# Streaming the tokens of three feed-forward products in blocks of 16, 128 and 4 from both halves in turn

## Chip, cores and metric

The kernel runs on one core of one Trainium2 chip. The metric is the device time in microseconds (us) of one execution. The kernel before takes 1833.14 us, the median of two runs (1832.73 and 1833.56 us).

## What is computed

A two-layer diffusion trunk over 256 latent tokens and 256 context tokens, width 1024. Each layer has a feed-forward half step, a pair of parallel mixers (attention and a short convolution) and a second feed-forward half step. The change touches only the first product of the feed-forward steps:

```python
def swiglu(h, wi, wo):
    a, g = jnp.split(h @ wi, 2, axis=-1)
    return (jax.nn.silu(g) * a) @ wo
...
    x = x + 0.5 * mod[:, 2] * swiglu(modulate(rmsnorm(x, norm_w[0]), mod[:, 0], mod[:, 1]), ffn1_wi, ffn1_wo)
    xc = xc + 0.5 * modc[2] * swiglu(modulate(rmsnorm(xc, norm_w[0]), modc[0], modc[1]), ffn1_wi, ffn1_wo)
```

`wi` is 1024 x 5632 (2816 value columns `a`, 2816 gate columns `g`), `wo` is 2816 x 1024, all float32. There are four such steps. In the first three both streams go through (512 tokens), in the fourth only the 256 latent tokens.

## The kernel before

The program is written engine by engine, each engine's order by hand, with semaphores between them; no scheduler or planner moves anything.

**Data.** The activations lie transposed: `hH` and `hL` are [128, 8, 512], channel in the partition, eight chunks of channels, 512 tokens along the row: tokens 0 to 255 are the latent half, 256 to 511 the context half. A float32 value is kept as a high part (`hH`, type float32r) and a low part (`hL`), and so are the weights (`wH`, `wL`). A product is three matmuls, high by high, low by high and high by low: the helper `triple`, lines 585 to 587. In a matmul here the weights are the stationary operand (a weight load of 128x128, the engine PEld of the profile) and the tokens are the moving operand, up to 512 columns. The result goes to a PSUM bank, which holds exactly 512 float32 columns per partition, token by token.

**Weights.** SP loads pieces of 512 KB into a ring of four slots, `raw`. ScalarE rounds a piece to `wH` (line 1071), VectorE subtracts to get `wL` (line 1355), TensorE uses it; `w_used` frees the slot.

**The stage of the change.** For feed-forward step `f` (0 to 3), `ffn` runs eleven groups of 256 value and 256 gate columns. The first group is `opening` (lines 642, 644, 654), which works with the norm before it and is not touched. Groups 1 to 10 are `group(i)`: four calls of `columns_piece`, one for each piece of weights. Each call goes over four channel chunks `kk` and two output banks and makes one `triple` for each, so 24 matmuls. The value product goes to banks 0 and 1, the gate product to banks 2 and 3. Their readers, on ScalarE and VectorE, take the banks after the last matmul, in token order. The steps 0, 1 and 2 of this count lie at 55.4 to 278.34, 743.54 to 966.47 and 1114.73 to 1337.66 us, with 960 matmuls of 512 columns each; step 3 (256 columns a matmul, tokens kept at 112 to 367 of the row) is at 1654.65 to 1764.34 us. Between every second group of steps 0 to 2 stand eight short records of `ada_reduce` (line 616), part of the modulation vectors.

**Other lines named below.** Line 956 weighs the values of the attention: its moving operand is `PT[:, 2 * r:2 * r + 2, kb * P:(kb + 1) * P]`, two runs of 128 columns out of two rows of `PT`; it gives 64 output columns for each `r`, and the two `r` run side by side. Line 598 is a small product at the start whose moving operand is one run of 256 columns and which runs four side by side. Both are float32, and a float32 matmul leaves two records in the trace. `last_rows` is the end of the feed-forward's second product, done by halves of 256 tokens.

Of the kernel before, what the change touches and what calls it, by code (L numbers as in the profile page):

```python
# [83 lines left out]
def span(t):  # L84

    at = SHORT_AT if t == SEQ else 0
    return slice(at, at + t)
# [32 lines left out]
def ada_batch(f, which):  # L120

    return next((b for b, (g, w, _, _) in enumerate(ADA_BATCHES) if (g, w) == (f, which)), None)
# [6 lines left out]
def ada_before(b):  # L129

    return sum(count for _, _, _, count in ADA_BATCHES[:b])
# [18 lines left out]
def build(nc, x, c, ctx, c_ctx, w_ada, b_ada, norm_w, ffn1_wi, ffn1_wo, w_in, conv_w, sink, w_oa, w_ob, w_out,  # L150
          ffn2_wi, ffn2_wo, final_norm_w, consts, out):
    stack = ExitStack()
    with stack:
        def sb(name, shape, dt=F32):
            return stack.enter_context(nc.sbuf_tensor(name, shape, dt))
# [6 lines left out]
        with ExitStack() as r:  # L162
            r.enter_context(nc.sbuf_tensor("h_lead", [P, LEAD], F32))
            hH = r.enter_context(nc.sbuf_tensor("hH", [P, DC, TOK], F32R))
            hL = r.enter_context(nc.sbuf_tensor("hL", [P, DC, TOK], F32R))
# [7 lines left out]
        wH = sb("wH", [P, RING, PIECE], F32R)  # L173
        wL = sb("wL", [P, RING, PIECE], F32R)
# [64 lines left out]
        ps = [stack.enter_context(nc.psum_tensor(f"ps{i}", [P, TOK], F32)) for i in range(4)]  # L239
# [65 lines left out]
        def halves(t):  # L305
            return t // SEQ
# [94 lines left out]

        BUSY = (2, 5, 5)

        FIN_DVE, FIN_ACT = (0, 1, 2, 3, 5, 6, 7), (4,)
        TURN = (0, 4, 5, 6, 7, 1, 2, 3)

# [7 lines left out]
        block = stack.enter_context(nc.Block())  # L414
# [164 lines left out]
        def _(pe):  # L579
            mm = nc.tensor.matmul  # L580

            def triple(dst, wa, wb, ra, rb, start, stop, group_check=True):

                kw = {} if group_check else {"skip_group_check": True}
                mm(dst, wa, ra, start=start, stop=False, **kw)  # L585
                mm(dst, wa, rb, start=False, stop=False, **kw)  # L586
                return mm(dst, wb, ra, start=False, stop=stop, **kw)  # L587

            def ada_sums(q):

                wait(pe, row_out, q)
                for k in range(DC):
                    if k % 4 == 0:
                        pe.wait_ge(ada0_loaded[2 * q + k // 4], 32)
                    for h in range(2):
                        g = 2 * (k % 2) + h
                        at = h * TOK + q % 2 * SEQ
                        last = mm(ps[5][32 * g:32 * g + 2, 0:SEQ], cact[:, :, k], ada0[8 * (q // 2) + k][:, at:at + SEQ],
                                  start=(k < 2), stop=(k >= DC - 2), skip_group_check=True)
                last.then_inc(ada_used, 1)  # L600

            def ada_turn(n):

                pe.wait_ge(row_out, n + 1)
                wait(pe, ada_out, n if n < QUARTERS else 2 * n - QUARTERS)
                for q in range(2 if n < QUARTERS else 4):
                    last = nc.tensor.transpose(ps[6][:, q * P:(q + 1) * P], rowS[:, q * P:(q + 1) * P], ident)
                last.then_inc(ada_T, 1)

            def ada_reduce(src, steps, at, start=False):  # L610

                pe.wait_ge(acc_step, steps)
                for v in range(2):
                    for h in range(2):
                        g = 2 * v + h
                        last = mm(ps[5][32 * g:32 * g + 4, :], oneh[:, at:at + 4],  # L616
                                  src[:, v, h * TOK:(h + 1) * TOK], start=start, stop=True, skip_group_check=True)
                last.then_inc(ada_red, 1)

            def ada_reduce_late(b):  # L620

                pe.wait_ge(x_ready, x_count(b, DC - 1, 1))
                for u in range(2):
                    ada_reduce(acc[:] if u == 0 else acc2[:], 2 * DC * (ada_before(b) + u + 1), 3 - u, start=(u == 0))
# [62 lines left out]
                        if kk == 6 and j == 2 and v in (1, 3):  # L687
                            ada_turn(QUARTERS + v)

            def columns_piece(n0, j, banks, kh, t, i=0, cs=None, rows=(hH, hL)):  # L690

                cs = slice(0, t) if cs is None else cs

                s = (n0 + j) % RING
                pe.wait_ge(lo_done, i * 4 + (n0 + j + 1))
                for k in range(4):
                    kk = 4 * kh + k
                    ws = [slice(k * 2 * P + b * P, k * 2 * P + (b + 1) * P) for b in range(2)]
                    for b, w in enumerate(ws):
                        last = triple(ps[banks + b][:, 0:t], wH[:, s, w], wL[:, s, w], rows[0][:, kk, cs], rows[1][:, kk, cs],  # L700
                                      kk == 0, kk == DC - 1, False)
                last.then_inc(w_used, 1)

# [127 lines left out]
            def second_norm(v):  # L831

                return {(0, 1, "within"): lambda: mean_squares(v, 1), (0, 2, "within"): lambda: spread_roots(v, 1)}

            def ffn(f, v):

                l, name = f // 2, "12"[f % 2]
                t = T_NORM[v]
                n0 = FIRST["wi" + name, l]

                def first_group():

                    if n0 > 0:
                        opening(n0, v, (t, t), second_norm(v) if halves(t) == 2 else {},
                                (lambda: ada_reduce_late(v)) if v == 3 else None)
                        return

                    opening(n0, v, (t, t), {1: lambda: ada_turn(1), 3: lambda: ada_turn(2), 5: lambda: ada_turn(3)},
                            None, {1: lambda: ada_sums(1), 3: lambda: ada_sums(2), 5: lambda: ada_sums(3)})

                def group(i, turn=None):


                    pe.wait_ge(a_out, i * 2 + 2 * GROUPS * f)
                    for j in range(4):
                        if j == 1:
                            pe.wait_ge(g_silu, i * 2 + 2 * GROUPS * f)
                        columns_piece(n0, j, 2 * (j % 2), j // 2, t, i, span(t))
                        if turn is not None and j == 1:
                            ada_turn(turn)  # L860

                b = ada_batch(f, "wi")
                first_group()
                if b is None:
                    with pe.Fori(1, GROUPS) as i:
                        group(i)
                else:
                    pe.wait_ge(oneh_set, 1)
                    pe.wait_ge(bank5_zero, f + 2)
                    for p in range(4):  # L870
                        group(2 * p + 1)
                        group(2 * p + 2)
                        ada_reduce(acc[:], 2 * DC * (ada_before(b) + p + 1), 3 - p, start=(p == 0))
                    group(GROUPS - 2, QUARTERS + b)
                    group(GROUPS - 1)
                n0 = FIRST["wo" + name, l]
                if b is not None:
                    pe.wait_ge(ada_out, QUARTERS + 2 * (b + 1))

                def bank_wait(m):  # L880
                    if m == 4:
                        pe.wait_ge(a_out, 2 * GROUPS * (f + 1))
                    if m == 6:
                        pe.wait_ge(g_silu, 2 * GROUPS * (f + 1))
                pe.wait_ge(g_lo, 2 * GROUPS * (f + 1) - 2)
                for j in range(RING):
                    rows_piece(n0, j, j, GH, GL, t, j == 0, False, bank_wait=bank_wait if j == 0 else None)
                with pe.Fori(1, FC // RING) as i:
                    for j in range(RING):
                        rows_piece(n0, j, i * RING + j, GH, GL, t, False, False, i)  # L890
                pe.wait_ge(g_lo, 2 * GROUPS * (f + 1))
                last_rows(n0, FC - 2, GH, GL, t, v + 1)
# [128 lines left out]
            for hf, came in enumerate((in_x, in_ctx)):  # L1021
                pe.wait_ge(came, 16)
                for b in range(4):
                    wait(pe, x_ready, 4 * hf + b - 3)
                    for m in (2 * b, 2 * b + 1):
                        for tb in range(2):
                            last = nc.tensor.transpose(ps[b][:, (m % 2) * SEQ + tb * P:(m % 2) * SEQ + (tb + 1) * P],
                                                       xin[:, 2 * hf + tb, m * P:(m + 1) * P], ident)
# [6 lines left out]
            for l in range(DEPTH):  # L1035
                last = nc.tensor.transpose(ps[6][:, 96 + 72 * l:96 + 72 * (l + 1)], vin[0:72, 1 + l, :],
                                           ident[0:72, 0:72])
# [834 lines left out]
```

## Time and profile before

| what | value |
|---|---|
| median of the runs | 1833.14 us (1832.73, 1833.56) |
| span of the profiled execution, first to last instruction | 1832.8 us |
| TensorE (PE) busy | 1818.3 us, 99% |
| VectorE (DVE) busy | 1121.4 us, 61% |
| ScalarE (ACT) busy | 693.6 us, 38% |
| DMA queue of the weights, share of 16 engines | 35.8% |

The profile shows one execution. It states no time of its own besides the span; the span lies 0.3 us below the median of the runs. Busy time is counted per engine; for PE the matmuls are pipelined, so that a matmul is listed with 0.39 us though the next one starts 0.227 us after it. The distance from start to start is what a matmul costs in a dense stream.

### The profile page before, as it was taken

To read this page: it belongs to the slowest core of one execution; us is meant where nothing else is said; L and a number is where in the kernel's file an instruction comes from. 1 tells how busy PE (TensorE), PEld (TensorE's weight loads), DVE (VectorE), ACT (ScalarE), POOL (GpSimd) and SP (SyncE) were. 2 spreads that over 40 slices of the span, in tenths; PEclk is the share of its full clock that TensorE was granted. 3 is DMA by queue.
4 is the path that set the end of the run, shared out by engine and by line. 5 is a ranking of instruction groups with operands and counts; after the bars stand their busy time and mean duration, and the time that the engine had idled before them with its cause. 6 is when DMAs were issued, how large, how long until landed. Compare 5 with 4: busy or idle time off the path is not lost.

```text
span 1832.8 us, 26314 instructions
## 1 busy us (share of the span) xinstructions
PE 1818.3 (99%) x10131; PEld 1543.2 (84%) x10131; DVE 1121.4 (61%) x1506; ACT 693.6 (38%) x1093; POOL 99.3 (5%) x174
## 2 busy tenths in 40 slices
PE   9999999999999999999999999999999999999998
PEld 6888888888777789888888888888888888999998
DVE  5877737556554366877737557777422487676554
ACT  3433332244334324433332144333322365556543
POOL 0101001010000001000001010000000100000000
PEclk9999999999999999999999999999999999999999
DMA  9766526423222323666527435565222254546663
GB/s 335 227 189 189 155 92 232 146 70 102 74 78 70 92 80 127 185 191 188 159 92 229 149 115 172 176 196 169 92 94 101 69 150 139 150 143 202 195 195 115
DMA packets 187893, 271.49 MB, mean 148 GB/s; under 512 B 25388, under 2 KB 154908, under 8 KB 187804
## 3 DMA queue, kind: packets, MB, share of 16 engines
q1 hardware_dynamic: 168912, 202.74, 35.8%
q0 software_dynamic: 18432, 67.12, 12.0%
q8 instruction: 64, 1.05, 0.2%
q10 hardware_dynamic: 460, 0.39, 0.1%
q14 instruction: 25, 0.20, 0.0%
HBM read 269.16 MB, written 1.05 MB: 147 GB/s over the span
## 4 chain that ended last, share of the span: by engine, by line
PE 94%; DVE 3%; ACT 2%; issue 1%; DMA 0%; SPq 0%; ACTq 0%; DVEq 0%
PE ps L585 23%; PE ps L586 23%; PE ps L587 23%; PE turned L586 2%; PE turned L587 2%; PE turned L585 2%; PE scored L585 2%; PE scored L586 2%; PE scored L587 2%; PE ps L642 2%; PE ps L644 2%; PE ps L654 2%; PE turned L956 1%; PE turned L939 1%; PE scored L925 1%; PE scored L616 1%
## 5 line engine op out<-in xcount | busy, mean ns | idle before, releaser
L1355 DVE TENSOR_TENSOR wL<-raw,wH 128x1024 fp32r<-128x1024 f32 x364 | 443.3, 1223 | 447.4 <-ACT wH L1071 447.1
L1071 ACT ACTIVATE wH<-raw 128x1024 fp32r<-128x1024 f32 x364 | 383.1, 1057 | 663.8 <-PE ps L587 658.4
L585 PE MATMUL ps<-hH,wH 128*128 128x512 f32 (+1 forms) x1592 | 583.0, 366 | 0.6 <-ACT T L1164 0.6
L586 PE MATMUL ps<-hL,wH 128*128 128x512 f32 (+1 forms) x1592 | 578.5, 363 | 0.0
L587 PE MATMUL ps<-hH,wL 128*128 128x512 f32 (+1 forms) x1592 | 578.4, 363 | 0.0
L585 PEld LDWEIGHTS ps<-hH,wH 128*128 128x128 f32 x1592 | 299.0, 188 | 64.7 <-issue 16.3
L587 PEld LDWEIGHTS ps<-hH,wL 128*128 128x128 f32 x1592 | 298.9, 188 | 48.3
L586 PEld LDWEIGHTS ps<-hL,wH 128*128 128x128 f32 x1592 | 299.0, 188 | 46.5
L585 PE MATMUL ps<-GH,wH 128*128 (+2 forms) x376 | 131.5, 350 | 0.0
L587 PE MATMUL ps<-GH,wL 128*128 (+2 forms) x376 | 131.2, 349 | 0.0
L586 PE MATMUL ps<-GL,wH 128*128 (+2 forms) x376 | 131.2, 349 | 0.0
L1402 DVE SCALAR_TENSOR_TENSOR acc<-adaC,cact,acc 128x1024 f32<-128x1024 f32 x96 | 118.8, 1278 | 0.0
L1183 ACT ACTIVATE T<-ps 128x512 f32<-128x512 f32 (+1 forms) x88 | 43.1, 541 | 154.6 <-PE ps L587 148.9
L1171 ACT ACTIVATE GH<-T 128x512 f32 (+3 forms) x88 | 49.4, 579 | 114.1 <-DVE T L1579 114.1
L585 PEld LDWEIGHTS ps<-GH,wH 128*128 128x128 f32 x376 | 70.8, 188 | 9.5
L586 PEld LDWEIGHTS ps<-GL,wH 128*128 128x128 f32 x376 | 70.8, 188 | 9.3
L587 PEld LDWEIGHTS ps<-GH,wL 128*128 128x128 f32 x376 | 70.7, 188 | 9.3
L560 POOL TENSOR_TENSOR T<-T 128x256 f32<-128x256 f32 x30 | 22.9, 764 | 969.8 <-ACT T L1076 968.9
L1579 DVE TENSOR_TENSOR T<-T 128x512 f32<-128x512 f32 (+1 forms) x88 | 50.8, 619 | 31.2 <-ACT T L1164 31.2
L1402 DVE SCALAR_TENSOR_TENSOR acc<-adaW,cact,acc 128x1024 f32<-128x1024 f32 x56 | 69.3, 1278 | 0.0
L585 PE MATMUL ps<-nearH,wH 128*128 128x256 f32 x240 | 68.8, 287 | 0.0
L642 PE MATMUL ps<-hH,wH 128*128 128x256 f32 (+1 forms) x208 | 65.0, 332 | 2.8 <-ACT hH L1086 2.0
(249 smaller groups left out, 2509.4 us busy)
## 6 DMA issues: line engine op xcount, KB each, us to landing
raw<-in_ffn_wi SPq DMA_DIRECT2D x176, 512.0 KB, 3.9
raw<-in_ffn_wo SPq DMA_DIRECT2D x88, 512.0 KB, 3.4
raw<-in_w_in SPq DMA_DIRECT2D x60, 512.0 KB, 3.9
adaC<-in_w_ada POOLq DMA_DIRECT2D x48, 512.0 KB, 4.4
adaW<-in_w_ada POOLq DMA_DIRECT2D x32, 512.0 KB, 4.3
adaA<-in_w_ada POOLq DMA_DIRECT2D x24, 512.0 KB, 4.0
adaB<-in_w_ada POOLq DMA_DIRECT2D x24, 512.0 KB, 4.6
raw<-in_w_out SPq DMA_DIRECT2D x16, 512.0 KB, 3.3
```

The costliest lines, as they stand in the source:

```text
L585: mm(dst, wa, ra, start=start, stop=False, **kw)
L586: mm(dst, wa, rb, start=False, stop=False, **kw)
L587: return mm(dst, wb, ra, start=False, stop=stop, **kw)
L642: mm(ps[banks(j) + b][:, cols], wH[:, s, w], h_of(v)[0][:, kk, rows], start=(kk == 0 and cols.start == 0), stop=False, skip_group_check=True)
L644: mm(ps[banks(j) + b][:, cols], wL[:, s, w], h_of(v)[0][:, kk, rows], start=False, stop=False, skip_group_check=True)
L654: last = mm(ps[banks(j) + b][:, cols], wH[:, s, weights(j, kk % 4, b)], h_of(v)[1][:, kk, rows], start=False, stop=(kk == DC - 1), skip_gr ...
L1071: av(wH[:, s, :], raw[:, s, :], ACT.Copy).then_inc(hi_done, 1)
L1171: av(dst, T[:, 2 + b, 0:t], ACT.Copy).then_inc(g_hi, 1)
L1183: av(T[:, b, 0:t], ps[b][:, 0:t], ACT.Copy).then_inc(a_out, 1)
L1355: tt(wL[:, s, :], raw[:, s, :], wH[:, s, :].bitcast(F32), ALU.subtract).then_inc(lo_done, 1)
L1402: stt(dst[:, v, :], src, cact[:, v, k:k + 1], dst[:, v, :], ALU.mult, ALU.add).then_inc(acc_step, 1)
L1579: tt(T[:, 2 + b, 0:t], T[:, 2 + b, 0:t], T[:, b, 0:t], ALU.mult).then_inc(g_prod, 1)
```

## The change

`columns_piece` gets an argument `block`, and `in_turn` rewrites an operand of 512 columns from one run into runs of `block` columns, one from the latent half, one from the context half, and so on. It is applied to both moving operands and, alike, to the PSUM bank, so every token's result lands in the same column as before. The step decides the size: 16 in step 0, 128 in step 1, 4 in step 2; step 3 stays as it was. Weights, banks, their order, waits and every other engine's program stay.

```diff
+        BLOCKS = (16, 128, 4, None)
...
+            def in_turn(ap, block):
+
+                if block is None:
+                    return ap
+                return ap.rearrange("p (h c e) -> p c h e", h=2, e=block)
+
-            def columns_piece(n0, j, banks, kh, t, i=0, cs=None, rows=(hH, hL)):
+            def columns_piece(n0, j, banks, kh, t, i=0, cs=None, rows=(hH, hL), block=None):
...
-                        last = triple(ps[banks + b][:, 0:t], wH[:, s, w], wL[:, s, w], rows[0][:, kk, cs], rows[1][:, kk, cs],
+                        last = triple(in_turn(ps[banks + b][:, 0:t], block), wH[:, s, w], wL[:, s, w],
+                                      in_turn(rows[0][:, kk, cs], block), in_turn(rows[1][:, kk, cs], block),
                                       kk == 0, kk == DC - 1, False)
...
-                        columns_piece(n0, j, 2 * (j % 2), j // 2, t, i, span(t))
+                        columns_piece(n0, j, 2 * (j % 2), j // 2, t, i, span(t), block=BLOCKS[f])
```

On TensorE, the last matmuls of the opening of step 0 and the first of group 1, before (the bank, what is streamed and what is stationary, and the sizes of the output: partitions, then columns):

```order
L654 MATMUL ps2<-hL,wH 128x512
L654 MATMUL ps3<-hL,wH 128x512
L585 MATMUL ps0<-hH,wH 128x512
L586 MATMUL ps0<-hL,wH 128x512
L587 MATMUL ps0<-hH,wL 128x512
L585 MATMUL ps1<-hH,wH 128x512
L586 MATMUL ps1<-hL,wH 128x512
L587 MATMUL ps1<-hH,wL 128x512
```

The same place with the change:

```order
L656 MATMUL ps2<-hL,wH 128x512
L656 MATMUL ps3<-hL,wH 128x512
L587 MATMUL ps0<-hH,wH 128x16x2x16
L588 MATMUL ps0<-hL,wH 128x16x2x16
L589 MATMUL ps0<-hH,wL 128x16x2x16
L587 MATMUL ps1<-hH,wH 128x16x2x16
L588 MATMUL ps1<-hL,wH 128x16x2x16
L589 MATMUL ps1<-hH,wL 128x16x2x16
```

No matmul has moved; each of the 960 of step 0 now goes 16 times over two runs of 16 columns. The first matmuls of group 1 in step 1, with the change:

```order
L587 MATMUL ps0<-hH,wH 128x2x2x128
L588 MATMUL ps0<-hL,wH 128x2x2x128
L589 MATMUL ps0<-hH,wL 128x2x2x128
L587 MATMUL ps1<-hH,wH 128x2x2x128
L588 MATMUL ps1<-hL,wH 128x2x2x128
```

And those of step 2:

```order
L587 MATMUL ps0<-hH,wH 128x64x2x4
L588 MATMUL ps0<-hL,wH 128x64x2x4
L589 MATMUL ps0<-hH,wL 128x64x2x4
L587 MATMUL ps1<-hH,wH 128x64x2x4
L588 MATMUL ps1<-hL,wH 128x64x2x4
```

Again only the form differs: two times two runs of 128 columns, and 64 times two runs of 4. The number of runs in a matmul is 32 in step 0, 4 in step 1 and 128 in step 2 (one before).

## Rows read from the trace of the kernel before

**Rows 1.** The page's first part and its row of the granted clock

```profile
span 1832.8 us, 26314 instructions
PE 1818.3 (99%) x10131; PEld 1543.2 (84%) x10131; DVE 1121.4 (61%) x1506; ACT 693.6 (38%) x1093; POOL 99.3 (5%) x174
...
PEclk9999999999999999999999999999999999999999
```

**Rows 2.** The page's fourth part, the chain that ended last, by engine

```profile
PE 94%; DVE 3%; ACT 2%; issue 1%; DMA 0%; SPq 0%; ACTq 0%; DVEq 0%
```

**Rows 3.** Busy time in the four gate-and-value stages: span, engines, clock, DMA share

```profile
55.40:278.34 222.94, 222.94 (x998) 180.73 (x996) 146.47 (x147) 73.76 (x100) 14.78 (x28) 1.00 0.54 165
743.54:966.47 222.93, 222.93 (x998) 180.73 (x996) 146.56 (x147) 73.86 (x100) 14.79 (x28) 1.00 0.53 162
1114.73:1337.66 222.93, 222.93 (x997) 180.74 (x996) 147.34 (x148) 73.87 (x100) 14.77 (x28) 1.00 0.54 165
1654.65:1764.34 109.69, 109.08 (x963) 108.89 (x961) 63.54 (x81) 60.72 (x101) 0.00 (x0) 1.00 0.65 201
```

**Rows 4.** Groups of PE from 55.4 to 278.34 us: busy, mean ns, idle before

```profile
L585 PE MATMUL ps<-hH,wH 128*128 128x512 f32 x320 | 125.1, 391 | 0.0
L587 PE MATMUL ps<-hH,wL 128*128 128x512 f32 x320 | 124.5, 389 | 0.0
L616 PE MATMUL scored<-acc,oneh 128*4 128x512 f32 x32 | 4.2, 593 | 0.0
```

**Rows 5.** Timeline of PE, 512 columns, first and last of 19: start, duration

```profile
59.70 0.39 PE L586 MATMUL ps<-hL,wH 128*128 128x512 f32 x1
...
63.78 0.39 PE L586 MATMUL ps<-hL,wH 128*128 128x512 f32 x1
```

**Rows 6.** Timeline around 143 us, PE and PEld: start us, duration us

```profile
142.96 0.39 PE L585 MATMUL ps<-hH,wH 128*128 128x512 f32 x1
142.96 0.19 PEld L586 LDWEIGHTS ps<-hL,wH 128*128 128x128 f32 x1
143.18 0.39 PE L586 MATMUL ps<-hL,wH 128*128 128x512 f32 x1
...
143.73 1.04 PE L616 MATMUL scored<-acc,oneh 128*4 128x512 f32 x8
```

**Rows 7.** Timeline, 256 columns, three places, first and last of 36, 37, 38

```profile
387.73 0.28 PE L587 MATMUL scored<-GH,wL 128*128 128x256 f32 x1
...
391.93 0.28 PE L586 MATMUL turned<-GL,wH 128*128 128x256 f32 x1
...
1599.74 0.28 PE L587 MATMUL scored<-QH,wL 128*128 128x256 f32 x1
...
1603.98 0.28 PE L587 MATMUL ps<-YH,wL 128*128 128x256 f32 x1
...
1699.74 0.28 PE L585 MATMUL ps<-hH,wH 128*128 128x256 f32 x1
...
1703.93 0.28 PE L586 MATMUL ps<-hL,wH 128*128 128x256 f32 x1
```

**Rows 8.** Float32 matmuls of 256 columns: timeline, and the group of L956

```profile
525.59 1.95 PE L956 MATMUL turned<-PT,VT 128*64 128x256 f32 x16
...
36.06 1.05 PE L598 MATMUL scored<-xin,cact 128*2 128x256 f32 x16
...
L956 PE MATMUL turned<-PT,VT 128*64 128x256 f32 x160 | 19.9, 387 | 0.0
```

**Rows 9.** Waits from 55.4 to 278.34 us: us in all, times, longest

```profile
ACT wH L1071 <- PE ps L587: 66.9, 21, 4.4
DVE wL L1355 <- ACT wH L1071: 50.0, 33, 5.7
```

## The prediction, made before the changed kernel ran

> **What bounds the kernel now.** I read the page from the top. TensorE is busy for 1818.3 of 1832.8 us, and its granted clock is nine tenths or more in every slice [rows 1]. The chain that ended last lies to 94% on TensorE [rows 2]. So the kernel is as long as its matmuls, and a change of what one matmul costs goes straight into the time.
>
> Next I asked for the busy time of the four stages in which the gate and value products run. In the three stages of the change PE has no idle time at all, 222.94 of 222.94 us in the first, at a granted clock of 1.00, the 2.4 GHz level [rows 3]. VectorE, the next busiest, works 146.47 us of them. The waits of the first stage say the same from the other side: ScalarE waits 66.9 us for TensorE to free weight slots, and VectorE waits 50.0 us for ScalarE [rows 9]. Nobody holds TensorE up. If its matmuls got 6% faster, 222.94 us would become 210 us, still well above VectorE's 146 and with the DMA engines at 0.54 of their time [rows 3]; so a gain passes through in full, and a loss too, since there is no idle time to swallow it.
>
> Then the price of one matmul. The groups give 391 and 389 ns [rows 4], but that is a duration with the pipeline in it. The timeline gives the distance: 19 matmuls of 512 columns start between 59.70 and 63.78 us, 18 steps in 4.08 us, 226.7 ns each [rows 5]. 960 of them make 217.6 us of the stage's 222.9 us; the other 5.3 us are the short reductions between groups and what follows them. 512 columns at one column per clock of 2.4 GHz are 213.3 ns. The matmul costs 13.3 ns more, and this is all that any order of the columns could win.
>
> **What the change does to it.** It removes no instruction and adds none; the order of the matmuls, the banks and the waits stays. What changes is the walk through the tokens and through the bank: 32 runs a matmul in stage 0 (blocks of 16), 4 in stage 1 (128), 128 in stage 2 (4), against one run now. So the sum has three terms, each 960 times the change of one step of 226.7 ns, and nothing else. ScalarE and VectorE read the banks after the last matmul, each column where it was; they see no difference. No DMA is issued in another place.
>
> Does a jump between runs cost anything? The only matmuls of the trace whose moving operand has more than one run are those of L956, two runs of 128. There 16 records stand in 1.95 us, two side by side, so eight steps; with 387 ns for the last, a step takes (1.95 - 0.387) / 7 = 0.223 us. The records of L598 read 256 columns in one run, 16 in 1.05 us, four side by side, so four steps; with the same tail a step takes (1.05 - 0.387) / 3 = 0.221 us [rows 8]. One run or two costs the same, to about 2 ns. But both are float32 and take some two clocks per column, so a lost clock at the jump could hide there, and their output is written in one run. For a stream of one column per clock and for an output in short runs, the trace before has no row.
>
> The bounds, then. From below, no stage can gain more than the 13.3 ns: 12.8 us a stage, 38.4 us in all. From above, the 2 ns by which the two float32 steps can differ would be 3 x 2 = 6 ns a matmul in stage 1 (5.8 us), 31 x 2 = 62 ns in stage 0 (60 us) and 127 x 2 = 254 ns in stage 2 (244 us), together 309 us. Another far end is the pace of a float32 matmul: in L616 eight records of 512 columns stand in 1.04 us, four side by side [rows 6], so with 593 ns for the last [rows 4] a step takes 0.45 us, 0.22 us over the present one; all three stages at that pace would be 2880 x 0.22 = 634 us slower. Between ends so far apart I take the value of the nearest row, L956 against L598: a jump costs nothing. The three terms are zero, and the sum is 1832.8 us of span. The median of the runs shown lies 0.3 us above the span: 1833.1 us.
>
> One rule of the Trainium skill speaks against the change. The Trainium skill's page "PSUM — Partial Sum Buffer" (Specifications (TRN2)) says that any non-contiguous access pattern in PSUM slows matmuls significantly. The Trainium skill's page "Advanced Engine Details and Errata" (PSUM Cachelines) says the same but asks for best throughput only that every two consecutive elements be contiguous, and the shortest run here has four. By the strict reading all three stages get slower; by the mild one none does. No row before has an output in several runs, so the trace cannot say; the strict reading is a rival below.
>
> **The rivals.**
>
> *The stream meets the weight load less often: faster.* The load of the next weights starts in the same instant as the stream (142.96 and 142.96 us) [rows 6]. The 13.3 ns may be reads of the two that collide. For it: the same instruction of 256 columns takes three different prices without a change of form. From 387.73 us on, 35 steps take 4.20 us, 120.0 ns; at 1599.74 us 36 steps take 4.24 us, 117.8 ns; at 1699.74 us, where the tokens lie at 112 to 367 of the row, 37 steps take 4.19 us, 113.2 ns [rows 7]. Over the 106.7 ns of 256 clocks that is 13.3, 11.1 and 6.5 ns. Where operands lie, or when the load begins, does move a price that should be one number. Blocks of 16 and 4 let the stream go forward through each half at half the speed, which changes every meeting of the two; blocks of 128 change it little. If both stages lose the whole 13.3 ns, 2 x 12.8 = 25.6 us go: 1807.5 us. With half of it, 1820.3 us. Against it: 226.7 ns holds over all of stage 0 whatever slot and channel chunk is read, so nothing says that another walk would be better and not worse. The Trainium skill ("SBUF — State Buffer", Who interferes with whom) gives TensorE two separate read ports and says that it never waits on anyone; by that there is nothing to win, though three prices for one form do not look like it.
>
> *The same meetings become more frequent: a little slower.* A walk in step with the weight load may also meet it all the time. As a size I have only what it costs now, 13.3 ns, once more in the two stages: 25.6 us the other way, 1858.7 us.
>
> *Each switch from one half to the other costs a clock: slower.* The place is the walk of the moving operand and of the bank in stages 0 and 2. The price is one clock of 2.4 GHz, 0.417 ns, for each run: 32 + 4 + 128 = 164 runs, 68.3 ns over the three stages' matmuls, times 960 = 65.6 us, of which blocks of 4 make 51.2, of 16 12.8 and of 128 1.6 us. The time would be 1898.7 us. It decides the sign at any price over zero and passes 2% (36.7 us, about what a measurement of this kernel can tell from no change) from 0.23 ns a run. For it: the rows of L956 leave up to 2 ns a jump open, and at half the pace they could hide a clock. Against it: L956 shows no trace of a jump.
>
> *The output in runs halves the pace.* This is the strict reading of the rule above. In the rows it would be the 0.45 us step: about 2467 us. Nothing in the trace before speaks for it but that it isn't excluded.
>
> That the change does not do what it says can be left out: the order shows the new form in all 3 x 960 matmuls.
>
> **How the numbers follow.** No cost: 0.42. Faster by fewer meetings: 0.27. A little slower by more: 0.10. A clock or so a run: 0.17. Half pace: 0.04. The likeliest is 1833.1 us. The range goes from 1805, just below the faster rival with two stages won, to 1900, just above the slower rival at one clock a run; left out are a gain in all three stages, a dearer jump and the half pace, somewhat over 0.1. Faster by over 2% needs 36.7 of the 38.4 us that exist, 0.02. Slower by over 2% is the last two cases, 0.21. Within 2%: 0.77.
>
> **What would show it.** In the changed profile the same timeline should read 226.7 ns a step in the three stages, and each stage should last 222.9 us with PE busy throughout. If the meetings matter, stages 0 and 2 move and stage 1 stays. If jumps cost, the steps grow in the ratio 32 to 4 to 128, and stage 2 shows it first: 280 ns a step for one clock a run. If the output's form matters, all three move, even stage 1. I am wrong if any stage differs from 222.9 us by more than a microsecond; I am wrong about what bounds the kernel if a stage's step changes and the total doesn't follow.

## The result and the profile after

The changed kernel takes 1869.68 us, the median of two runs (1869.46 and 1869.90), against 1833.14 us: slower, with a ratio of 1.0186 and a 95% interval of 1.0157 to 1.0215. The loss is clear; whether it is more or less than 2% is not, since the interval holds 2%. My 1833.1 us was wrong, though the time lies in my range of 1805 to 1900 us.

The page of the changed kernel, first part:

```profile
span 1867.4 us, 26314 instructions
PE 1852.0 (99%) x10131; PEld 1545.1 (83%) x10131; DVE 1121.6 (60%) x1506; ACT 695.6 (37%) x1093; POOL 99.3 (5%) x174
...
PEclk9999999999999999999999999999999999999999
```

The same number of instructions and the same clock as in [rows 1], and PE still 99% busy. PE's busy time grew by 33.7 us, that of the other engines by 2 us at most. The four gate-and-value stages (span, then PE, PEld, DVE, ACT, POOL, granted clock, DMA share, GB/s), to set beside [rows 3]:

```profile
55.69:291.20 235.51, 235.51 (x998) 182.91 (x996) 146.49 (x147) 73.75 (x100) 14.78 (x28) 1.00 0.51 156
756.48:979.40 222.92, 222.92 (x997) 180.71 (x996) 146.55 (x147) 73.90 (x100) 14.78 (x28) 1.00 0.53 162
1127.66:1372.77 245.11, 245.11 (x997) 181.96 (x996) 147.44 (x148) 75.67 (x100) 14.78 (x28) 1.00 0.48 150
1689.30:1798.94 109.64, 109.19 (x962) 108.98 (x961) 63.53 (x80) 60.68 (x101) 0.00 (x0) 1.00 0.64 201
```

Against 222.94, 222.93, 222.93 and 109.69 us before, stage 0 (blocks of 16) grew by 12.6 us, stage 1 (blocks of 128) by nothing, stage 2 (blocks of 4) by 22.2 us, and stage 3, which is unchanged, by nothing. The sum is 34.8 us; the spans differ by 34.6. So the whole loss lies in two stages, and in them in the step of a matmul. The timeline of PE in stage 0 and stage 2, first and last row of 81 and of 78 matmuls in a row:

```profile
59.77 0.40 PE L589 MATMUL ps<-hH,wL 128*128 128x512 f32 x1
...
78.97 0.40 PE L588 MATMUL ps<-hL,wH 128*128 128x512 f32 x1
...
1131.66 0.42 PE L588 MATMUL ps<-hL,wH 128*128 128x512 f32 x1
...
1150.92 0.41 PE L587 MATMUL ps<-hH,wH 128*128 128x512 f32 x1
```

80 steps in 19.20 us are 240.0 ns, 77 steps in 19.26 us are 250.1 ns, where [rows 5] gave 226.7 ns. In clocks of 2.4 GHz: 544 before, 576 with blocks of 16, 600 with blocks of 4.

The medians differ by 36.5 us, the spans of the profiled executions by 34.6. The difference lies within the scatter of the executions of the kernel before, which the last experiment shows.

### The profile page after: what moved, and what is told of

It is laid out like the page before. It is cut to its first block, busy times and chain, and to the rows that moved or that the text cites. A ratio compares the mean times of both kernels' runs of the same rounds, so it can differ in the third digit from the quotient of the medians.

```text
span 1867.4 us, 26314 instructions
## 1 busy us (share of the span) xinstructions
PE 1852.0 (99%) x10131; PEld 1545.1 (83%) x10131; DVE 1121.6 (60%) x1506; ACT 695.6 (37%) x1093; POOL 99.3 (5%) x174
## 4 chain that ended last, share of the span: by engine, by line
PE 93%; DVE 4%; ACT 2%; issue 1%; DMA 0%; SPq 0%; ACTq 0%; DVEq 0%
PE ps L587 23%; PE ps L589 23%; PE ps L588 23%; PE turned L587 2%; PE turned L589 2%; PE turned L588 2%; PE scored L587 2%; PE scored L589 2%; PE scored L588 2%; PE ps L644 2%; PE ps L646 2%; PE ps L656 2%; PE turned L965 1%; PE turned L948 1%; PE scored L934 1%; PE scored L618 1%
## 5 line engine op out<-in xcount | busy, mean ns | idle before, releaser
L587 PE MATMUL ps<-hH,wH 128*128 128x512 f32 (+1 forms) x1592 | 595.6, 374 | 0.5 <-ACT T L1173 0.5
L588 PE MATMUL ps<-hL,wH 128*128 128x512 f32 (+1 forms) x1592 | 591.1, 371 | 0.0
L589 PE MATMUL ps<-hH,wL 128*128 128x512 f32 (+1 forms) x1592 | 591.0, 371 | 0.0
```

## How the experiments are read

Each experiment puts three variants into the three stages of one kernel, so the number that counts is the step of a matmul in a stage. One row per stage gives it. It lists the first matmuls of the triples (high by high), 320 in a stage, with the shortest, median and longest duration in ns and then the first and the last start in us. Before, those two starts are 222.3 us apart; what a stage has more, divided by the 957 steps between them, is added to 226.7 ns. The changed kernel's three rows:

```profile
L587 PE MATMUL ps<-hH,wH x320: 402/403/504, 55.7 to 290.5; 128*128 128x512 f32 x160
...
L587 PE MATMUL ps<-hH,wH x320: 389/389/504, 756.5 to 978.7; 128*128 128x512 f32 x160
...
L587 PE MATMUL ps<-hH,wH x320: 412/419/513, 1127.7 to 1372.0; 128*128 128x512 f32 x160
```

234.8 us less 222.3 over 957 is 13.1 ns, so 239.8; 222.2 us give 226.6; 244.3 us give 249.7. This agrees with the steps read one by one to 0.4 ns.

Before, the three stages last the same to 0.01 us, so what one has more is its variant's doing. The theories, as the expectations name them: A, the reads of the stream meet those of the weight load; B, the bank's form costs; C, every jump costs the same; later D, it costs to come back to the same part of the memory soon; E, the length of a run sets the price.

## Reading side or bank

`read_only` keeps the blocks on the tokens alone, `bank_only` on the bank alone; in both the results stand in permuted token columns.

```diff
-                        last = triple(in_turn(ps[banks + b][:, 0:t], block), wH[:, s, w], wL[:, s, w],
+                        last = triple(ps[banks + b][:, 0:t], wH[:, s, w], wL[:, s, w],
```

and for `bank_only`

```diff
-                                      in_turn(rows[0][:, kk, cs], block), in_turn(rows[1][:, kk, cs], block),
+                                      rows[0][:, kk, cs], rows[1][:, kk, cs],
```

> The changed kernel with only the moving operands walked in blocks of 16, 128 and 4; the bank is written in one run, so the results stand in permuted token columns. In the changed kernel the steps of a matmul are 240.0, 226.7 and 250.0 ns in the three stages, against 226.7 before. Theory A (the reads of the stream meet those of the weight load): 240.0, 226.7, 250.0 again, some 1867 us. Theory B (the bank's form costs): 226.7 in all three, 1833 us. Theory C (every jump of any operand costs a part): something between, for example 233 and 238.

> The changed kernel with only the bank walked in blocks, the tokens read in one run (results again in permuted columns). Theory A: 226.7 ns in all three stages, 1833 us. Theory B: 240.0, 226.7, 250.0 ns, 1867 us. Theory C: between.

`read_only`, stages 0 and 2:

```profile
L587 PE MATMUL ps<-hH,wH x320: 402/403/504, 55.6 to 290.4; 128*128 128x512 f32 x160
...
L587 PE MATMUL ps<-hH,wH x320: 412/419/513, 1127.6 to 1371.9; 128*128 128x512 f32 x160
```

`bank_only`, stages 0 and 2:

```profile
L587 PE MATMUL ps<-hH,wH x320: 389/389/504, 55.7 to 277.9; 128*128 128x512 f32 x160
...
L587 PE MATMUL ps<-hH,wH x320: 389/389/504, 1115.0 to 1337.3; 128*128 128x512 f32 x160
```

`read_only` is the changed kernel to the tenth of a microsecond, 234.8 and 244.3 us. `bank_only` is the kernel before, 222.2 and 222.3 us, though its bank is written in runs of 16 and of 4. The whole price of the change is paid where the tokens are read. Theory B is out for these three block sizes with a jump of 256 columns; the bank was not tried alone with others.

## The weight load

`narrow_64` is the changed kernel with stationary operands of 64 columns (the other columns are left out); a weight load is then listed with 137 ns in place of 190.

```diff
-                        last = triple(in_turn(ps[banks + b][:, 0:t], block), wH[:, s, w], wL[:, s, w],
+                        wn = slice(w.start, w.start + (64 if block is not None else P))
+                        last = triple(in_turn(ps[banks + b][0:wn.stop - wn.start, 0:t], block), wH[:, s, wn], wL[:, s, wn],
```

> The changed kernel with stationary operands of 64 columns in place of 128 in the three stages, so that a weight load is half as long; half of the value and gate columns are left out. Theory A: what a step costs over the 213.3 ns of 512 clocks comes from the weight load and halves: 240.0, 226.7, 250.0 become about 226.7, 220 and 232. Theory B or C: the extra of stages 0 and 2 over stage 1 stays 13.3 and 23.3 ns, whatever happens to the 13.3 ns that all have.

```profile
L587 PE MATMUL ps<-hH,wH x320: 402/403/479, 55.1 to 289.7; 128*64 128x512 f32 x160
...
L587 PE MATMUL ps<-hH,wH x320: 387/392/478, 755.7 to 980.7; 128*64 128x512 f32 x160
...
L587 PE MATMUL ps<-hH,wH x320: 407/417/488, 1129.7 to 1370.7; 128*64 128x512 f32 x160
```

239.6, 229.5 and 246.2 ns. A step of blocks of 16 costs the same with half the columns loaded, and the stage of blocks of 128, which should have become cheaper, got 2.9 ns dearer. Two more kernels went further: `narrow_run` reads the tokens in one run with stationary operands of 64, 32 and 8 columns, `narrow_8` has blocks of 16, 32 and 4 with 8 columns.

```diff
-        BLOCKS = (16, 128, 4, None)
+        BLOCKS = (None, None, None, None)
+
+        WIDTHS = (64, 32, 8, P)
```

> Tokens in one run as before, stationary operands of 64, 32 and 8 columns in the three stages (the other columns are left out). It asks where the 13.3 ns over 512 clocks come from. Theory A (the weight load's reads): 220, 217 and 214 ns. Theory C or D (the stream by itself): 226.7 ns in all three.

> Blocks of 16, 32 and 4 in the three stages with stationary operands of 8 columns, so that the weight load is next to nothing (the other columns are left out). With full weight loads these are 240.0, 236.7 and 250.0 ns. Theory A: 214 to 220 ns in all three. Theory D: the part that the walk itself costs stays; if the 13.3 ns of the single run are the weight load's, then about 227, 223 and 237 ns, if not, 240, 237 and 250.

`narrow_run`, and then `narrow_8`:

```profile
L589 PE MATMUL ps<-hH,wH x320: 387/392/478, 54.0 to 279.1; 128*64 128x512 f32 x160
...
L589 PE MATMUL ps<-hH,wH x320: 388/394/478, 745.0 to 971.5; 128*32 128x512 f32 x160
...
L589 PE MATMUL ps<-hH,wH x320: 387/389/478, 1120.5 to 1344.7; 128*8 128x512 f32 x160
```

```profile
L589 PE MATMUL ps<-hH,wH x320: 402/402/484, 55.7 to 290.1; 128*8 128x512 f32 x160
...
L589 PE MATMUL ps<-hH,wH x320: 395/402/476, 756.1 to 987.2; 128*8 128x512 f32 x160
...
L589 PE MATMUL ps<-hH,wH x320: 407/412/487, 1136.2 to 1377.0; 128*8 128x512 f32 x160
```

One run: 229.6, 231.1 and 228.7 ns; blocks of 16, 32 and 4: 239.3, 235.9 and 246.0 ns. With a sixteenth of the columns loaded, the 13.3 ns of the single run have not gone, and neither has most of the price of the blocks. That price did shrink, though: over a single run at the same width, blocks of 16 cost 10.6 ns in place of 13.1, blocks of 4 17.3 in place of 23.0. And a load of 8 columns is not next to nothing: `narrow_run` lists it with 88 ns. So theory A is out as far as the number of columns loaded goes, and with it the values that it gave; a meeting with some part of the load that doesn't shrink with the columns was not tested.

The load has a small hand in it all the same. `apart_run` and `apart_run2` leave the tokens in one run and take the stationary slice further along its row (with the wrong weights, then); `apart_16` and `apart_4` do so with blocks of 16 and 4 in all stages.

```diff
-                    ws = [slice(k * 2 * P + b * P, k * 2 * P + (b + 1) * P) for b in range(2)]
+                    at = [k * 2 * P + b * P + shift for b in range(2)]
+                    ws = [slice(a, a + P) if a + P <= PIECE else slice(shift, shift + P) for a in at]
```

> Tokens in one run as before, but the stationary slice is taken 16, 32 and 64 columns (64, 128, 256 bytes) further along the row of wH and wL in the three stages, so that weight load and stream start at other distances; the weights used are the wrong ones, the work is the same. Before, both rows begin at the same place modulo 512 bytes. Theory A (the reads of the stream meet those of the weight load by address): the 226.7 ns change, by up to 15 ns either way. Theory C (the walk of the stream costs by itself): 226.7 ns in all three stages, 1833 us.

> The same with 8, 96 and 112 columns. Theory A: three other values, 96 and 112 columns being 32 and 16 backwards modulo 128. Theory C: 226.7 ns in all.

> Blocks of 16 in all three stages, the stationary slice shifted by 16, 32 and 64 columns. Theory A: with blocks of 16 stream and weight load go along their rows at the same speed, so their distance stays what it is at the start and the shift must matter most: from about 213 ns where they never meet to well over the 240 ns of no shift. Theory C: 240.0 ns in all three stages, 1872 us.

> Blocks of 4 in all three stages, the stationary slice shifted by 16, 32 and 64 columns. Theory A: as with blocks of 16, values that differ between the stages, some below 226.7 ns. Theory C: 250.0 ns in all three, about 1900 us.

`apart_run` (16, 32, 64 columns):

```profile
L589 PE MATMUL ps<-hH,wH x320: 393/398/502, 55.4 to 283.8; 128*128 128x512 f32 x160
...
L589 PE MATMUL ps<-hH,wH x320: 390/393/504, 749.7 to 977.6; 128*128 128x512 f32 x160
...
L589 PE MATMUL ps<-hH,wH x320: 389/389/504, 1126.5 to 1348.8; 128*128 128x512 f32 x160
```

`apart_run2` (8, 96 and 112 columns) has 228.4, 227.8 and 224.3 us in place of the 222.3 of before. `apart_16`, the first two stages:

```profile
L589 PE MATMUL ps<-hH,wH x320: 402/402/504, 54.2 to 289.0; 128*128 128x512 f32 x160
...
L589 PE MATMUL ps<-hH,wH x320: 402/403/504, 755.0 to 989.8; 128*128 128x512 f32 x160
```

| shift of the weights, columns | 0 | 8 | 16 | 32 | 64 | 96 | 112 |
|---|---|---|---|---|---|---|---|
| tokens in one run, ns | 226.7 | 233.1 | 233.1 | 232.5 | 226.7 | 232.5 | 228.8 |
| blocks of 16, ns | 239.8 | | 239.8 | 239.8 | 239.8 | | |
| blocks of 4, ns | 249.7 | | 252.0 | 249.8 | 249.7 | | |

The single run does change with the distance, by up to 6.4 ns, and only upward; of the seven distances tried, that of the kernel before has the lowest price, together with a shift of 64. Blocks of 16, for which I had expected the largest effect since the two walks then keep their distance, don't move at all; blocks of 4 move by 2.3 ns at most. Theory A failed where it was most definite.

## Length of the runs or length of the jumps

`sizes_8_32_64` changes the length alone, with jumps of 256 columns as in the changed kernel (the edit is the table `BLOCKS`).

> Both operands in turn, with blocks of 8, 32 and 64 in place of 16, 128 and 4. Theory A (the walk through each half goes at half speed, in step with the weight load, as long as the block is short against what the weight load covers meanwhile): 8 close to 16 and 4, 240 to 250 ns; 32 about 240; 64 between 226.7 and 240. Theory C with a price per jump (13.3 ns for the 31 jumps of blocks of 16, 0.43 ns each): 8 gives 254 ns, though blocks of 4 gave 250 and not 281; 32 gives 233, 64 gives 230.

```profile
L587 PE MATMUL ps<-hH,wH x320: 403/406/512, 55.9 to 293.8; 128*128 128x512 f32 x160
...
L587 PE MATMUL ps<-hH,wH x320: 397/400/504, 759.8 to 991.5; 128*128 128x512 f32 x160
...
L587 PE MATMUL ps<-hH,wH x320: 389/389/504, 1140.4 to 1362.7; 128*128 128x512 f32 x160
```

243.0, 236.5 and 226.7 ns. Blocks of 64 are free; from there the price rises, but per jump it falls. That is against a fixed price per jump, theory C. It made me think of places 64 columns apart as one part of the memory, and so to vary the jump. `strides_16`, `strides_4`, `strides_32` and `sizes_2_8` do so with another table, of the number of parts and the block:

```diff
-        BLOCKS = (16, 128, 4, None)
+        BLOCKS = ((16, 16), (8, 16), (4, 16), None)
...
-                return ap.rearrange("p (h c e) -> p c h e", h=2, e=block)
+                return ap.rearrange("p (h c e) -> p c h e", h=block[0], e=block[1])
```

> Blocks of 16 in all three stages, but the walk jumps by 32, 64 and 128 columns where the changed kernel jumps by 256: 32 jumps or nearly so in each. Known by now: blocks of 64 and 128 cost nothing, and shifting the weights by 64 columns changes nothing for a single run, as if places 64 columns (256 bytes) apart were the same part of the memory. Theory D (it costs to come back to the same part soon): a jump of 32 columns never goes to the same part at once, so it is cheaper than the 240 ns of the changed kernel, about 233 ns; jumps of 64 and 128 go to the same part every time, where the changed kernel does so every second time, so 250 ns or more for both. Theory C (each jump costs the same): 240 ns in all three stages.

> Three stages: blocks of 2 from halves 256 columns apart; blocks of 8 with jumps of 64 columns; blocks of 8 with jumps of 128. Measured so far with jumps of 256: 226.7 ns for blocks of 64 and 128, 236.7 for 32, 240.0 for 16, 243.3 for 8, 250.0 for 4. Theory D (a place comes back too soon): the distance decides, as with blocks of 16, where 128 gave 231.2 and 64 gave 239.4; so about 243 and 233 for the blocks of 8. Theory E (the length of a run decides): 243 for both, and blocks of 2 go on with the row, 260 ns or more.

> Blocks of 4 with jumps of 8, 64 and 128 columns in the three stages; with jumps of 256 it is 250.0 ns. Theory E: 250 ns in all three. Theory D: about 250 for 64, clearly less, 235 to 240, for 128; for jumps of 8 the walk stays near and goes forward twice as fast, so it is the cheapest, near 227.

> Blocks of 32 with jumps of 64 and of 128 columns, and blocks of 64 with jumps of 128. With jumps of 256, blocks of 32 cost 236.7 and of 64 226.7 ns. Theory E: 236.7, 236.7, 226.7. Theory D: about 236 for jumps of 64, below 231 for 128, 226.7 for the last.

`strides_16` (jumps of 32, 64, 128), then `strides_4` (8, 64, 128), then `sizes_2_8` (blocks of 2 with 256, of 8 with 64 and 128):

```profile
L587 PE MATMUL ps<-hH,wH x320: 398/402/517, 56.1 to 290.9; 128*128 128x512 f32 x160
...
L587 PE MATMUL ps<-hH,wH x320: 395/402/504, 756.8 to 991.0; 128*128 128x512 f32 x160
...
L587 PE MATMUL ps<-hH,wH x320: 387/387/502, 1140.0 to 1366.5; 128*128 128x512 f32 x160
```

```profile
L587 PE MATMUL ps<-hH,wH x320: 392/392/500, 55.8 to 282.1; 128*128 128x512 f32 x160
...
L587 PE MATMUL ps<-hH,wH x320: 433/442/542, 748.0 to 1018.1; 128*128 128x512 f32 x160
...
L587 PE MATMUL ps<-hH,wH x320: 427/437/532, 1167.2 to 1428.7; 128*128 128x512 f32 x160
```

```profile
L587 PE MATMUL ps<-hH,wH x320: 496/503/593, 55.4 to 380.0; 128*128 128x512 f32 x160
...
L587 PE MATMUL ps<-hH,wH x320: 387/402/524, 846.3 to 1080.8; 128*128 128x512 f32 x160
...
L587 PE MATMUL ps<-hH,wH x320: 392/394/507, 1229.8 to 1456.1; 128*128 128x512 f32 x160
```

All steps together, in ns, by block (down) and jump (across), both in columns of 4 bytes:

| block | 8 | 32 | 64 | 128 | 256 |
|---|---|---|---|---|---|
| 2 | | | | | 333.6 |
| 4 | 230.9 | | 276.6 | 267.7 | 249.7 |
| 8 | | | 239.4 | 230.9 | 243.0 |
| 16 | | 239.8 | 239.1 | 231.1 | 239.8 |
| 32 | | | 236.4 | 233.1 | 236.5 |
| 64 | | | | 226.7 | 226.7 |

Down the last column, the change's own jump, the price goes up with every halving of the block. That speaks for the length. (`strides_32` gave the row of 32 its jumps of 64 and 128 and the row of 64 its jump of 128: 231.6, 228.4 and 222.3 us from first to last start.) But theory E alone is wrong: blocks of 4 cost 230.9 or 276.6 ns as the jump is 8 or 64. Theory D in my form is wrong too: it gave 233 ns for blocks of 16 with jumps of 32 (239.8 measured), and 250 ns or more for jumps of 64 and 128 (239.1 and 231.1). Written anew after the blocks of 16 had been seen, it was right that 128 is cheaper than 256 for blocks of 8 and 32, and wrong for blocks of 4, where it gave 235 to 240 ns and 267.7 were measured.

Two limits of this table. The walk always covers 512 columns, so a shorter jump also means more places visited in turn (2 with a jump of 256, 4 with 128, 8 with 64); the runs can't separate the jump from that number. And both operands were walked alike; that the bank is free was shown only for jumps of 256 and blocks of 4, 16 and 128.

`base_off` moved the tokens by 32 bytes, so that each block of 16 straddles two pieces of 64 bytes (if the tokens' row began at a multiple of 64 bytes before, which no view shows):

```diff
-            r.enter_context(nc.sbuf_tensor("h_lead", [P, LEAD], F32))
+            r.enter_context(nc.sbuf_tensor("h_lead", [P, LEAD // 2], F32))
...
-        BLOCKS = (16, 128, 4, None)
+        BLOCKS = (16, None, 4, None)
```

> Blocks of 16, one run and blocks of 4 as before, with hH and hL 32 bytes (8 columns) nearer to the start of the row, so that a block of 16 straddles two pieces of 64 bytes. If reads come in aligned pieces of 64 bytes, blocks of 16 touch twice as many and rise from 240 to 250 ns or more, and blocks of 4 stay at 250. If only the run's length or distance counts (theory E or D): 240 and 250 stay. The single run shows the phase: 226.7 to 233 ns, as when the weights were shifted.

```profile
L587 PE MATMUL ps<-hH,wH x320: 401/403/505, 55.3 to 290.1; 128*128 128x512 f32 x160
...
L587 PE MATMUL ps<-hH,wH x320: 392/396/504, 761.0 to 989.4; 128*128 128x512 f32 x160
...
L587 PE MATMUL ps<-hH,wH x320: 405/416/520, 1138.5 to 1386.0; 128*128 128x512 f32 x160
```

239.8 ns for blocks of 16, unchanged, so under that condition it isn't the number of aligned 64-byte pieces. The single run goes to 233.1 ns, as it does when the weights are shifted by the same 8 columns. Blocks of 4 go to 253.0, where every theory had 250.

## Can blocks ever win

No stage of 512 columns in any run is below the 226.7 ns of the kernel before, so nothing there points to a version that beats it. One place remained where a single run isn't at its best: the 120.0 ns of [rows 7]. `halves_walk` is the kernel before, with blocks there and in the last feed-forward step:

```diff
+        HALF = {1: 64, 2: 32, 3: 16}
...
-                            last = triple(ps[bank_of(m)][:, side(hf)], wH[:, s, ws], wL[:, s, ws], ra[:, kk, rows],
-                                          rb[:, kk, rows], False, kk == k + 1, False)
+                            e = HALF.get(v)
+                            last = triple(in_turn(ps[bank_of(m)][:, side(hf)], e), wH[:, s, ws], wL[:, s, ws],
+                                          in_turn(ra[:, kk, rows], e), in_turn(rb[:, kk, rows], e),
+                                          False, kk == k + 1, False)
```

> The three stages of the change as before it, in one run. Instead blocks are tried where a matmul has only 256 columns: in the last pieces of three products that are worked by halves of 256 tokens (96 matmuls each, 120.0 ns a step before), blocks of 64, 32 and 16 whose partner lies 128 columns on, the fourth such place left as it is; and in the gate and value products of the last feed-forward step (960 matmuls, 113.3 ns) blocks of 64. If a walk with blocks can also save reads, the 120.0 ns fall towards 113.3, at most 2 us in all. If blocks only cost, as in all runs so far, blocks of 64 change nothing, those of 32 and 16 bring the step to about 122 to 127 ns, and the time is that of before within 2 us.

It took 1835.02 us, median of 10, against 1839.94, median of 13. The ratio is put at 0.999 with an interval of 0.9972 to 1.0007: no difference that this could tell. Its timeline at the first place (blocks of 64, first and last of 35), at the second (blocks of 32, of 36), at the third (blocks of 16, of 35) and in the last feed-forward step (blocks of 64, of 36):

```profile
387.80 0.28 PE L590 MATMUL scored<-GL,wH 128*128 128x256 f32 x1
...
391.88 0.28 PE L591 MATMUL turned<-GH,wL 128*128 128x256 f32 x1
...
706.82 0.28 PE L591 MATMUL scored<-hH,wL 128*128 128x256 f32 x1
...
710.98 0.28 PE L590 MATMUL turned<-hL,wH 128*128 128x256 f32 x1
...
1075.82 0.28 PE L589 MATMUL scored<-GH,wH 128*128 128x256 f32 x1
...
1079.89 0.28 PE L590 MATMUL turned<-GL,wH 128*128 128x256 f32 x1
...
1699.83 0.28 PE L589 MATMUL ps<-hH,wH 128*128 128x256 f32 x1
...
1703.95 0.28 PE L591 MATMUL ps<-hH,wL 128*128 128x256 f32 x1
```

34 steps in 4.08 us are 120.0 ns, 35 in 4.16 us are 118.9, 34 in 4.07 us are 119.7; before, the three places have 119.7 to 120.0. So the expected 122 to 127 ns for blocks of 32 and 16 did not come: at 256 columns these blocks cost nothing, where at 512 columns and the same jump of 128 they cost 6.4 and 4.4 ns. No run shows why.

In the last feed-forward step, 35 steps in 4.12 us are 117.7 ns, where [rows 7] had 113.2. The blocks need not be the reason: the same step, left as it was before, stands in the traces of other experiments with either price. Here are the changed kernel and `strides_32`, both with one run of 256 columns there:

```profile
L587 PE MATMUL ps<-hH,wH x320: 276/276/380, 1689.3 to 1798.6; 128*128 128x256 f32 x160
...
L587 PE MATMUL ps<-hH,wH x320: 276/281/384, 1668.4 to 1781.9; 128*128 128x256 f32 x160
```

From first to last start that is 109.3 and 113.5 us, at a granted clock of 1.00 in both. Six profiles with this step untouched have 113.5 us, the others, the kernel before among them, 109.3. So blocks of 64 cost nothing here either. The two prices also fit most of the scatter of the whole kernel. Five of the 13 executions of the kernel before in this comparison took 1832.45 to 1835.01 us and eight 1838.94 to 1840.78, and 4.4 ns on the 1488 matmuls of the last feed-forward step are 6.5 us. No profile of one of the longer executions of the kernel before is there to show it directly. The two medians above fall into different ones of the two groups. What makes an execution take the one price or the other is not shown. The stages of 512 columns are the same under both, 222.3 us in one run.

## Why the prediction was wrong

**The bound** was read rightly. PE is 99% busy before and after, and 34.8 us more in two stages made the span 34.6 us longer. No other engine hid any of it, and the bank's readers saw no difference.

**The step that failed** is the one in which I took the value between the ends: "I take the value of the nearest row, L956 against L598: a jump costs nothing." The measured terms are 12.6, 0 and 22.2 us in place of three zeros. The row of L956 was right for what it had in it, two runs of 128: blocks of 128 cost nothing at full pace too (226.6 ns). I carried it over to runs of 16 and of 4, which it does not bound, and I had written myself that its half pace could hide a clock. What the runs showed in its place: read in blocks of 16 the matmul costs 13.3 ns more, in blocks of 4 23.3 ns more, on the reading side alone. By my own sign, a stage off by more than a microsecond, two of the three terms were wrong.

**The slower rival** had the right sign and the right stages, and of its two places, tokens and bank, one is right. I gave it 0.17. Its one clock a run was exact for blocks of 16 (32 runs, 32 clocks, 12.8 us forecast and 12.6 measured), too high for 128 (1.6 against 0) and more than twice too high for 4 (51.2 against 22.2: 56 clocks for 128 runs). So its total of 65.6 us was mis-sized; the price is not per jump, and the exact hit at 16 is luck.

**The rivals about the weight load**, 0.27 and 0.10, are not borne out: the changed kernel's price stays for the most part when far fewer columns are loaded. The second had a size near the truth, 25.6 us, by accident. What I read out of [rows 7] was half right: the price of a run depends on where the operands lie, as the shifted weights show (226.7 to 233.1 ns). It does not follow that the load is what the 13.3 ns are made of; with 8 columns they are still there. What I held against this rival, the same 226.7 ns for every slot and chunk, was no evidence: slots and chunks lie multiples of 128 columns apart, and a shift of 64 already changes nothing. The Trainium skill ("SBUF — State Buffer", Who interferes with whom) with its separate ports comes nearer to this than I did. But the shift of the weights, 226.7 to 233.1 ns, shows that the load is not without influence, and there the measurement decides.

**The output's form**, 0.04, is out. By the strict reading of the Trainium skill ("PSUM — Partial Sum Buffer", Specifications (TRN2)) all three stages had to slow; `bank_only` writes its bank in runs of 16, 128 and 4 at 226.6 to 226.7 ns. The trace agrees with the mild reading ("Advanced Engine Details and Errata", PSUM Cachelines), for runs of four columns and more. On the reading side the Trainium skill ("Advanced Engine Details and Errata", SBUF Cachelines) asks for at least two hits on a line of 16 bytes. A block of 4 has four hits on such a line if it starts on one, and it still costs 249.7 ns with the change's jump; the measurement decides.

**The far end** of 634 us was misread. A float32 matmul leaves two records, so the 0.45 us were the step of a record; a matmul would take 0.9 us, and the far end would be some three times as far. The forecast did not use it.

**The time around the span** I put at 0.3 us, from the median. The changed kernel's profiled execution took 1869.46 us with a span of 1867.4, so 2.1 us lie around it, and the executions of before in the experiments show the same (1834.29 us with 1832.2). The profiled execution of before, with its span of 1832.8 us, was then not one of the two runs that the median is made of.

**What stays open** is what the price is made of. Shown are: it is paid by the read of the moving operand; it doesn't depend on the bank's form; fewer columns in the weight load take away between a fifth and somewhat over a quarter of it; with jumps of 256 columns it rises as runs shorten below 64 columns. Not explained are the dependence on the jump, above all for blocks of 4, the free blocks at 256 columns, and the 32 clocks that a single run of 512 costs over its 512.

## What to carry to other kernels

In a dense stream of float32r matmuls of 512 columns, keep the moving operand in runs of 64 columns or more, and put any reordering on the PSUM side, where runs down to 4 columns were free. With 256 columns a matmul, measure first: blocks of 16 and 32 cost nothing there. When a change varies a parameter over stages, look for the row that bounds the shortest or smallest value of it; if there is none, the term is unknown, and a price of nothing has to be argued for like any other. Putting one variant into each of several equal stages gives three measurements in one run.

## What the runs showed that I had not expected

Writing a bank in 128 runs of 4 columns costs nothing. Walking tokens and bank in blocks of 4 costs from 4 to 50 ns a matmul depending on the jump and with it the number of places visited in turn, and blocks of 2 cost 107 ns. The single run too has several prices, 226.7 to 233.1 ns for 512 columns, set by the distance between stationary and moving rows modulo what seems to be 64 columns (shift 0 and 64 alike, 32 and 96 alike). And the same 256-column step, in the same place of the program and at the same clock, takes 113.3 ns in some executions and 117.7 in others.
